# Order of the query blocks in a block-sparse attention stage: the two blocks that keep all their keys come first

## The reference

```python
def attend(args):
    qa, qi, wi, t0 = args
    q_pos = t0 + jnp.arange(Q_BLOCK)
    causal = key_pos[None, :] <= q_pos[:, None]
    logits = jnp.einsum('bqhd,bsd->bqhs', qi.astype(f32), k_idx)
    score = jnp.einsum('bqh,bqhs->bqs', wi.astype(f32), jax.nn.relu(logits))
    score = jnp.where(causal[None], score, -jnp.inf)
    _, idx = lax.top_k(score, topk)
    c_sel = jax.vmap(lambda c, i: c[i])(c_kv, idx).astype(f32)
    valid = idx <= q_pos[None, :, None]
    s = jnp.einsum('bqhr,bqkr->bhqk', qa.astype(f32), c_sel)
    s = jnp.where(valid[:, None], s, -jnp.inf)
    p = jax.nn.softmax(s, axis=-1)
    return jnp.einsum('bhqk,bqkr->bqhr', p, c_sel)
```

## Time and profile before

| | us |
|---|---|
| median of three runs | 4329.13 |
| profiled execution | 4329.46 |
| its span | 4327.6 |
| PE busy | 3948.2 (91%) |
| DVE busy | 2670.0 (62%) |
| ACT busy | 2122.4 (49%) |
| POOL busy | 1206.8 (28%) |
| granted clock, mean | 0.955 |

### The profile page before, as it was taken

One profiled execution on the slowest core, in us unless ns is written; L12 is line 12 of the kernel. 1 busy time (PEld: TensorE's weight loads), 2 busy tenths in 40 slices (PEclk: granted clock), 3 DMA queues, 4 the chain that ended last, 5 costly groups with the idle time before them and its releaser, 6 DMA issues. The chain is left out here.

```text
span 4327.6 us, 76198 instructions
## 1 busy us (share of the span) xinstructions
PE 3948.2 (91%) x31096; PEld 2780.6 (64%) x31096; DVE 2670.0 (62%) x5092; ACT 2122.4 (49%) x3127; POOL 1206.8 (28%) x966
## 2 busy tenths in 40 slices
PE   7989999777888899888789899898999999999989
PEld 5767776445666666666568687686555555555567
DVE  5555555455777787878675423245677777777543
ACT  4444444397778888777533323222333333333431
POOL 1111111126344444435111000000444444444200
PEclk9999999887999999999889999999999999999999
DMA  3334233402111121211256544456232323231243
GB/s 125 98 111 131 81 101 102 123 21 50 34 37 40 42 53 35 54 48 48 81 172 196 186 147 146 168 212 181 56 75 56 74 67 73 58 74 40 95 144 107
DMA packets 388093, 404.95 MB, mean 94 GB/s; under 512 B 115776, under 2 KB 287488, under 8 KB 387488
## 3 DMA queue, kind: packets, MB, share of 16 engines
q1 hardware_dynamic: 386656, 396.77, 31.1%
q10 hardware_dynamic: 1088, 3.32, 0.2%
HBM read 248.36 MB, written 151.62 MB: 92 GB/s over the span
## 5 line engine op out<-in xcount | busy, mean ns | idle before, releaser
L142 ACT ACTIVATE PT<-psum 128x1024 f32<-128x1024 f32 x384 | 394.3, 1027 | 658.3 <-PE psum L132 657.7
L170 DVE TENSOR_REDUCE m<-psum 128x1 f32<-128x1024 f32 x384 | 468.0, 1222 | 273.4 <-PE psum L132 273.4
L132 PE MATMUL psum<-xc,wah 128*128 128x512 f32 x1600 | 515.4, 404 | 3.2 <-DVE xc L146 2.9
L146 POOL TENSOR_TENSOR part<-PT 128x1024 f32<-128x1024 f32 x144 | 341.7, 2373 | 471.7 <-DVE all L146 379.1
L132 PE MATMUL psum<-PT,V 128*64 128x512 f32 x1536 | 371.5, 605 | 0.0
L146 POOL TENSOR_TENSOR Lm<-gm,cst 64x512 f32<-64x512 f32 x192 | 258.7, 1347 | 356.5 <-PE psum L132 194.3
L143 ACT ACTIVATE bias<-score,cand,cols 128x2048 bf16<-128x2048 f32 (+6 forms) x217 | 314.6, 1450 | 86.5 <-DVE cand L153 80.2
L132 PEld LDWEIGHTS psum<-xc,wah 128*128 128x128 f32 x1600 | 300.2, 190 | 79.6 <-issue 10.3
L143 ACT ACTIVATE sgn<-score,cand,cols 128x1920 bf16<-128x1920 f32 (+6 forms) x217 | 291.3, 1342 | 88.1 <-DVE cand L153 83.5
L132 PE MATMUL psum<-hc,w4h 128*128 128x512 f32 x1024 | 320.0, 394 | 8.7 <-DVE w4l L146 8.7
L132 PE MATMUL psum<-xc,wal 128*128 128x512 f32 x800 | 316.0, 395 | 0.0
(11 more groups left out here) (336 smaller groups left out, 8663.9 us busy)
## 6 DMA issues: line engine op xcount, KB each, us to landing
raw_a<-in_w_a SPq DMA_DIRECT2D x50, 512.0 KB, 4.0
raw_w<-in_w_in SPq DMA_DIRECT2D x32, 512.0 KB, 5.3
QNh<-scr_qnh SPq DMA_DIRECT2D x48, 256.0 KB, 5.0
QRh<-scr_qrh SPq DMA_DIRECT2D x96, 128.0 KB, 4.5
QNl<-scr_qnl SPq DMA_DIRECT2D x48, 256.0 KB, 6.2
xin<-in_x SPq DMA_DIRECT2D x16, 512.0 KB, 4.1
scr_AR<-AR SPq DMA_DIRECT2D x32, 256.0 KB, 2.2
scr_BK<-BK SPq DMA_DIRECT2D x32, 256.0 KB, 2.2
```

What stands on the lines that cost most here:

```text
L132: return self.e.matmul(out, a, b, start=start, stop=stop, skip_group_check=True)
L142: return self.e.activation(out, src, f, bias=bias, scale=scale)
L146: return self.e.tensor_tensor(out, a, b, op) if self.e else self.vector(out)
L170: return self.e.tensor_reduce(out, a, AX, op, negate=negate) if self.e else self.vector(a)
```

## The change

`nth` now gives b = 0 number 0, b = 1 number 1, and b = 2 to 15 the numbers 15 down to 2. The waits for the block two places earlier are adapted where that block has no selection, the wait of nobias for an earlier block's scores falls away for b < 3, and the preload of x and y of the next phase hangs on the last block (number 2) and waits for the selections of the last two blocks and the last tie piece. Nothing is added to or removed from the work of any engine.

```diff
+        FEW = TOPK // 128
+
         def nth(b):
 
-            return NT - 1 - b
+            return b if b < FEW else NT - 1 + FEW - b
...
                 elif what == "qx":
                     b = k[1]
-                    if b > 1:
+                    if b - 2 >= FEW:
                         q.wait_ge(x_pe, "log", b - 2, last_of[b - 2], 1)
...
-                    if nth(b) == 1:
-                        q.wait_ge(k_act, "in", b - 2)
+                    if b == NT - 1:
                         q.wait_ge(k_act, "in", b - 1)
+                        q.wait_ge(k_act, "in", b)
+                        q.wait_ge(k_pool, "tie", b, last_of[b])
                         q.wait_ge(d_yo, 6)
...
-                    elif b > 1:
+                    elif b - 2 >= FEW:
                         q.wait_ge(k_pool, "tie", b - 2, last_of[b - 2])
...
-                            if b > 1:
+                            if b - 2 >= FEW:
                                 q.wait_ge(k_act, "in", b - 2)
...
-                    q.wait_ge(t_dve, "score", b - 3, 3, last_of[b - 3], 1)
+                    if b > 2:
+                        q.wait_ge(t_dve, "score", b - 3, 3, last_of[b - 3], 1)
```

## The result

The changed kernel took **4340.56 us** (median of 11 runs, 4336.23 to 4345.90), the kernel before beside it on the same chip 4330.55 us (11 runs). The ratio is 1.0019, 95% interval 1.0011 to 1.0027: slower, clear of the noise but small (the medians differ by 10.0 us). The forecast was 4340.5. That it was met to the tenth is luck: four of its five terms were off, by 9 to 12 us each, two up and two down, and cancel; so the total confirms little. The profiled execution took 4336.63 us (span 4334.8, before 4327.6).

The account below looks back on a forecast made before the run. The prediction took ACT as nearly full in the first selection and PE, DVE and ACT as running in lockstep in the body. Terms 40 + 5 - 3 + 0 - 31 = +11 us on 4329.5 gave 4340.5, range 4318 to 4360.

Parts of the forecast that it names:

- What leaves the end: End of the second phase: without the two small blocks it ends with the 384-key block, -31 us (-32 to -24).
- First term: Start of the second phase: ACT's first pass over the 2048-key block's scores comes 40 us later (25 to 55).
- three more are 16 us: Start: three more levels of the recurrence's inverse ahead of PE's last score piece, claimed to cost 16 us.
- The lower end of 25: Start, to ACT's first pass: 20 tiles and 5 us, if the inverse's levels run under the score pieces.
- Second term: From ACT's first pass to the 2048-key block's threshold: +5 us (0 to +14), from passes, copies and exps on ACT.
- the upper end of 14: First pass to threshold: +14 us if small-block products in DVE's queue wait for PE and hold up flips.
- The third rival of the forecast: Small blocks' steps stall the in-order DVE and ACT queues: 50 + 10 - 3 - 31 = +26, 4355.5 us; chance 0.12.
- Third term: Ties, from the last selection pass to the first masked score: -3 us (-15 to +5), less recurrence work on POOL.
- The body: First masked score of the 2048-key block to that of the 384-key block: 0, with 10 us either side.
- Same time, by the clock: Start and ties: small blocks fill PE's gap and keep its clock up, +4 us, 4333.5; chance 0.22.
- Faster, by cover: Start: levels run under score pieces, ties shed all that left them; -19 us, 4310.5; chance 0.18.
- Slower by more: Start: DVE and ACT queues stall at small blocks' steps, +26 us, 4355.5; decided above 1095 for first masked score; chance 0.12.

Follow-up runs that it names:

- x4: Small blocks first as in the change, but kT and vv tiles woven with the first selection as in the kernel before; 4310.6 us, 0.9948 of the kernel before.

## Why the prediction was right, point by point

**What leaves the end, -31.** Right: -32.4. The cover held too: the three loads of y went out at 2161.8, 23 us ahead of the last output, and the next phase's first matmul comes 7.5 us behind that output, 8.1 before.

**First term, +40: measured +28.3.** The part that failed most is "three more are 16 us". The timeline of PE has the levels' first products here:

```profile
872.33 0.97 PE L132 MATMUL psum<-Xl,Lm 64*64 64x64 f32 x26 [0.42 <-POOL Lm L146]
...
877.66 1.15 PE L132 MATMUL psum<-Xl,Lm 64*64 64x64 f32 x32
...
883.13 1.15 PE L132 MATMUL psum<-Xl,Lm 64*64 64x64 f32 x32
...
887.70 1.15 PE L132 MATMUL psum<-Xl,Lm 64*64 64x64 f32 x32
```

They are 5.3, 5.5 and 4.6 us apart, the step I took from the earlier trace rows. But a level that takes 5 us end to end is mostly waiting between three products of about 1.1 us, and PE filled it: it was busy 60.2 of 62 us up to 897. I added up a chain's length where I should have added PE's busy time. The groups of PE from the first tile to the last score of the 2048-key block, before (835.7 to 865.2 us) and now (836 to 892.9), give it; first the tiles:

```profile
L132 PE MATMUL psum<-P,pt 128*128 128x512 f32 x8 | 6.4, 889 | 12.2 <-DMA P<-scr_ckvT 11.4 <-ACT kT L142 0.8
L132 PE MATMUL psum<-pt,P 128*128 128x512 f32 x7 | 4.1, 652 | 0.0
```

```profile
L132 PE MATMUL psum<-P,pt 128*128 128x512 f32 x32 | 17.1, 677 | 11.4 <-DMA P<-scr_ckvT 11.4
L132 PE MATMUL psum<-pt,P 128*128 128x512 f32 x32 | 14.7, 595 | 0.0
```

The tiles are 21 us more of PE. My 20 was nearly right for the wrong count: only 7 of the 32 tiles (two matmuls each; the eighth begins at the cut) stood ahead of the last score before, not 12, since five more ran while ACT and DVE finished the scores; so 25 moved, at less than the 1.0 us that I took for one. The levels' three products are 12.4 us in the same groups, against 3.3 before: 9 us more where I had 16. The small block's pieces are 2 us where I had 4, and some 2 us come back because the scores and the recurrence's first products ran faster than before. (Recorded times overlap, so these sum to 30; PE's stretch up to the last score grew from 29.5 to 56.9 us.) The lower end of 25 described this case.

**Second term, +5: measured +14.2.** The count of passes was right: 15 for the 1920-key block stand ahead of the threshold, and the experiment with it held back prices each at 1.9 us. Missing were the waits, which I had put at nothing. The groups of ACT from 897.4 to 1027:

```profile
L143 ACT ACTIVATE bias<-score,cand,cols 128x2048 bf16<-128x2048 f32 x31 | 64.7, 2088 | 9.3 <-DVE cand L153 9.0
L143 ACT ACTIVATE sgn<-score,cand,cols 128x1920 bf16<-128x1920 f32 x15 | 29.6, 1974 | 0.0
L142 ACT ACTIVATE rl<-psum 128x512 f32<-128x512 f32 (+1 forms) x16 | 8.2, 569 | 3.0 <-PE psum L132 2.9
...
L143 ACT ACTIVATE P<-P,mx 128x256 f32<-128x256 f32 (+1 forms) x12 | 5.5, 463 | 0.0
```

Taken from start to start, the twelve exps are 5.9 us with their accumulator reads (I took 5; a read of 0.19 us starts before its exp's record ends, and two exps of 0.39 us start 0.39 us apart, at 899.34 and 899.73). The four passes more are 8 us, the ten kT copies fewer 5.2 (I took 5.7). ACT waits 9.0 us for cand against 5.0 over the same passes in the earlier trace rows, and 2.9 us for PE's index scores against 0.7: with 0.8 at a level's copy, some 7 of the 9 us that were missed. The longest wait for cand, 2.5 us, ends at 948.86; DVE shows what stood ahead of the flip:

```profile
945.62 0.69 DVE L146 TENSOR_TENSOR Xl<-Xl,psum 128x512 f32<-128x512 f32 x1 [1.42 <-PE psum L132]
947.76 0.69 DVE L146 TENSOR_TENSOR Xu<-Xu,psum 128x512 f32<-128x512 f32 x1 [1.46 <-PE psum L132]
948.37 0.21 DVE L153 TENSOR_SCALAR flip<-cols 128x1 int32<-128x1 f32 x1
```

ACT's pass had ended at 945.6. So it is a hold-up in DVE's queue, for which the upper end of 14 stood, but at this longest one DVE stands at two pieces of the recurrence, not at the small blocks' products that the forecast had looked to; the others were not followed up. The third rival of the forecast ("in-order queues stall", +50 and +10) named this mechanism; it cost some 7 us in this term, where the rival gave it 5, but the first term came out 12 below the forecast's and not 10 above.

**Third term, -3: measured -12.5.** The first and the last tie operation on POOL, before and now:

```profile
998.55 1.52 POOL L152 TENSOR_SCALAR rl<-bias 128x512 f32<-128x512 bf16 x1
...
1039.54 1.93 POOL L153 TENSOR_SCALAR bias<-rl 128x512 bf16<-128x512 f32 x1
```

```profile
1036.83 1.52 POOL L152 TENSOR_SCALAR rl<-bias 128x512 f32<-128x512 bf16 x1 [1.26 <-ACT score L143]
...
1069.85 1.93 POOL L153 TENSOR_SCALAR bias<-rl 128x512 bf16<-128x512 f32 x1
```

Two things failed. The masks ahead of the first tie operation, for which I had set up to +5 against the term, gave 4.5 us: before, POOL was still at an Xu and two masks when the selection ended (993.9), and began 4.7 us later; now its masks were done while ACT was still selecting, and it waits 1.3 us for ACT. The other 8 us lie between the two operations, 41.0 us before and 33.0 now. Four masks and the six operations that left are 13 us of POOL, more than the 10 I had allowed, but 5 of them come back as waits, since POOL now stands idle for DVE's scan in every chunk:

```profile
L146 POOL TENSOR_TENSOR Lm<-gm,cst 64x512 f32<-64x512 f32 x4 | 5.1, 1264 | 0.3
L146 POOL TENSOR_TENSOR rl<-rl,bias 128x512 f32<-128x512 f32 x4 | 4.6, 1154 | 8.9 <-DVE rl L158 8.9
```

POOL is busy 41.8 of 47 us before and 25.0 of 35 now: it had paced the ties, and now shares that with DVE.

**The body, 0: measured +8.7.** The step that failed is the count of pieces as the measure: "269 pieces instead of 267" was right, and said nothing. Where in the body they stand matters. With the recurrence's spreading undone the same kernel has a body of 1069.5, 20 us shorter, and a time 27 us lower; the kernel before with the early spreading has 1096.3, 15.5 us longer, though only 4.3 us of time. Both parts of the body moved: its first three stages 350.2 to 344.1, the rest 730.5 to 745.4.

**The rivals.** *Same time, by the clock:* not borne out where it was placed. From 951 us to the first masked score the granted clock was 0.65, 0.50 and 0.63, below the 0.71 of the earlier trace rows, and the tie stretch had 0.63 where it had 0.79. The gap did not fill: PE was busy 39 of 76 us up to 1027, although the small blocks' last value product came only at 1012.5, because their products there are few. The Trainium skill ("TensorE: Matmul & The Clock Gate", Part 1, What's actually happening) says that the array's clock follows how busy the engine has been. This trace does not contradict it, nor does it test what a filled gap would have given. *Faster, by cover:* its two conditions both came true (the levels ran under the scores, the ties shed all), but the second term stood at its other end and the body took 9. Its deciding point, a first masked score below 1063, was missed by 9 us. *Slower by more:* 1095 was far off. Of the forecast's own signs, the body (within 10 us of 1081) and the last output (24 us behind it) came true; the first pass (897.4, for 900 to 920) and the first masked score (1071.8, for 1075 to 1090) were just outside.

So the forecast holds in sign and size, and of its reasons the end, the tiles' price and the count of passes hold. It charged the levels by their length, put the waits at nothing, gave the ties too little, and overlooked that moving the small blocks also moves the recurrence. Both faster kernels (4310.6 and 4313.5) repair one of these two, the tiles' place or the recurrence's. They don't add up: with both the time is 4313.9, not told apart from either.

## What to carry to other kernels

When a static order is made by weaving lists by weight, an edit to one list moves the others: compare where the pieces of each list stand along the whole body, not only how many there are. For a stretch in which one engine is full, price work by that engine's instructions, and a chain of dependent steps elsewhere by the busy time it takes from the full engine, not by its length. When a later job shares an in-order engine with the one that everything waits on, count how many of its steps stand ahead of the first one's end. And test the new place of moved work without the work: here the start was faster with the small blocks in it than without, because they kept the second selection back.

## What the runs showed of the hardware

The granted clock at the head of the body differed between kernels with nearly the same share of PE busy. In the first stage (first masked score to the 1920-key block's last tie) of the kernel before, then of the changed kernel:

```profile
1041.50:1127.50 86.00, 75.52 (x974) 49.96 (x974) 64.49 (x170) 63.88 (x76) 40.71 (x33) 0.88 0.15 36
```

```profile
1071.80:1157.30 85.50, 74.78 (x1003) 49.85 (x1000) 67.48 (x172) 65.69 (x80) 41.44 (x33) 0.96 0.14 34
```

PE is busy 0.88 and 0.87 of the time and was granted 0.88 and 0.96, although the stretch ahead of it had the lower clock in the changed kernel (0.63 against 0.79). Over the first three stages a matmul takes 72.7 ns of busy time before (312.15 us for 4296) and 69.7 ns now (305.33 for 4383). Part of that is the mix, since the 87 more are small ones; the index scores alone (kidx, qx) take 716 and 661 ns.

I did not find out what the clock follows here, and part of it may not belong to the kernels at all: runs of one kernel differ too. The eleven runs of the changed kernel had a mean granted clock of 0.951 to 0.956, and the two lowest times (4336.2 and 4336.6 us) came with 0.955 and 0.956, the highest (4345.9) with 0.951. The six runs of x4 go from 4298.7 us at 0.962 to 4317.2 at 0.957. A stage's clock was read in one execution of each kernel.
